# First feed-forward product with one 512-column pass per weight block, its halves summed at eviction, and conditioning units spread over two stages

## The reference

```
hn = rms_norm(h, g_ffn_pre[i])
f_gate, f_up = jnp.split(hn @ w_ffn_in[i], 2, axis=-1)      # 1024 -> 2 x 2816
f = (jax.nn.silu(f_gate) * f_up) @ w_ffn_out[i]             # 2816 -> 1024
h = h + rms_norm(f, g_ffn_post[i])
```

```
cond = jax.nn.silu(c)
mod = cond @ w_ada[layer] + b_ada[layer]                    # 1024 -> 6 x 1024
```

## Time and profile before

| | us |
|---|---|
| median of 3 runs | 1114.41 (1113.29 to 1114.71) |
| the profiled execution | 1109.89 |
| its span | 1108.1 |
| PE busy | 1014.9 (92%) |
| PEld busy | 764.6 (69%) |
| DVE busy | 505.7 (46%) |
| POOL busy | 493.3 (45%) |
| ACT busy | 379.1 (34%) |

### The profile page before, as it was taken

One profiled execution on the slowest core, in us unless ns is written; L12 is line 12 of the kernel. 1 busy time (PEld: TensorE's weight loads), 2 busy tenths in 40 slices (PEclk: granted clock), 3 DMA queues, 4 the chain that ended last, 5 costly groups with the idle time before them and its releaser, 6 DMA issues.

```text
span 1108.1 us, 18626 instructions
## 1 busy us (share of the span) xinstructions
PE 1014.9 (92%) x7938; PEld 764.6 (69%) x7938; DVE 505.7 (46%) x905; ACT 379.1 (34%) x540; POOL 493.3 (45%) x209
## 2 busy tenths in 40 slices
PE   7999999999999999999999999899988777878776
PEld 6989988788799999887898896344444333434332
DVE  2998987566457676214345544232232221212113
ACT  7345545643563344446595432000000000000002
POOL 6987799867786878988565510000000000000000
PEclk9999999999999999999999999999999999989999
DMA  9554455456569889858443879999999999999995
GB/s 366 210 190 156 154 191 208 166 202 235 197 250 336 313 348 360 314 190 331 133 151 121 326 322 419 413 426 425 427 427 425 425 427 426 427 427 424 425 424 210
DMA packets 38533, 342.07 MB, mean 309 GB/s; under 512 B 4273, under 2 KB 4657, under 8 KB 6322
## 3 DMA queue, kind: packets, MB, share of 16 engines
q1 hardware_dynamic: 37152, 337.56, 76.3%
q10 hardware_dynamic: 1298, 3.32, 0.9%
HBM read 339.81 MB, written 1.05 MB: 308 GB/s over the span
## 4 chain that ended last, share of the span: by engine, by line
PE 57%; DMA 26%; DVE 6%; POOL 6%; ACT 2%; SPq 2%; issue 1%; DVEq 0%; ACTq 0%; another core or an unknown queue 0%
DMA ring<-in_gu 17%; PE ps L521 12%; PE ps L523 12%; PE ps L522 12%; PE ps L1141 6%; POOL spl L2432 6%; DMA raw<-in_stream 5%; PE ps L1188 5%; DMA ring<-in_dn 3%; PE ps L1177 2%; SPq L2489 2%; PE ps L1121 1%; ACT sph L1245 1%; PE ps L514 1%; DVE ps L1960 1%
## 5 line engine op out<-in xcount | busy, mean ns | idle before, releaser
L2432 POOL TENSOR_TENSOR spl<-raw,sph 128x1024 fp32r<-128x1024 f32 x204 | 492.9, 2450 | 153.9 <-ACT sph L1245 153.9
L1245 ACT ACTIVATE sph<-raw 128x1024 fp32r<-128x1024 f32 x204 | 206.9, 1054 | 160.8 <-DMA raw<-in_stream 101.9
L521 PE MATMUL ps<-xbh,sph 128*128 128x256 f32 x480 | 137.0, 285 | 4.9 <-DVE xbl L1777 2.0
L522 PE MATMUL ps<-xbl,sph 128*128 128x256 f32 x480 | 136.0, 283 | 0.0
L523 PE MATMUL ps<-xbh,spl 128*128 128x256 f32 x480 | 136.0, 283 | 0.0
L2366 DVE TENSOR_TENSOR ar<-ar,ps 64x256 f32<-64x256 f32 x32 | 13.5, 423 | 262.2 <-ACT ar L1705 262.2
L1705 ACT ACTIVATE ar<-ps 64x256 f32<-64x256 f32 x32 | 12.1, 377 | 329.8 <-PE ps L1141 329.8
L1188 PE MATMUL ps<-ar,ar 128*128 128x512 f32 x256 | 119.8, 611 | 0.0
L521 PEld LDWEIGHTS ps<-xbh,sph 128*128 128x128 f32 x480 | 92.2, 192 | 6.3 <-DVE ar L2116 2.2
L521 PE MATMUL ps<-xah,sph 128*128 128x256 f32 x320 | 92.1, 288 | 1.1 <-DVE xal L1767 0.8
L522 PEld LDWEIGHTS ps<-xbl,sph 128*128 128x128 f32 x480 | 92.2, 192 | 0.0
(11 more groups left out here) (310 smaller groups left out, 1626.1 us busy)
## 6 DMA issues: line engine op xcount, KB each, us to landing
raw<-in_stream SPq DMA_DIRECT2D x127, 1024.0 KB, 5.1
ring<-in_gu SPq DMA_DIRECT2D x46, 2048.0 KB, 44.6
ring<-in_dn SPq DMA_DIRECT2D x22, 2048.0 KB, 44.6
ring<-in_gu SPq DMA_DIRECT2D x24, 1024.0 KB, 10.8
ring<-in_dn SPq DMA_DIRECT2D x14, 1024.0 KB, 9.2
ar<-in_gu SPq DMA_DIRECT2D x7, 1024.0 KB, 25.9
slotx<-in_gu SPq DMA_DIRECT2D x5, 1024.0 KB, 38.7
ar<-in_dn SPq DMA_DIRECT2D x3, 1024.0 KB, 47.8
```

Of the source, the lines that this page charges most:

```text
L521: e.matmul(o, sh, mh, start=start, stop=False)
L522: e.matmul(o, sh, ml, start=False, stop=False)
L1245: e.activation(u.half(SPH[u.n % NSP], h), u.half(RAW[u.slot], h), ACTF.Copy).then_inc(w.up(hi_ok), 1)
L2432: e.tensor_tensor(u.half(SPLO[u.n % NSP], h), u.half(RAW[u.slot], h), u.half(SPH[u.n % NSP], h), ALU.subtract).then_inc(w.up(lo_ok), 1)
```

## The change

- The planned stream has one ada unit in each of the 11 steps, two in steps 3 and 7 (13 instead of 20), and one ada unit before each of w0 to w8 (9 instead of 2).
- The activations' high and low parts (`XB`) become one tensor with a part index. `two_sided` takes the place of `fm_unit` for the gate and up units: per block one matmul of 512 columns (high weight times high and low activation side by side) and one of 256 columns (low weight times high activation) on top of the first half. A unit now fills a pair of banks, one bank for each half of 128 features, and each bank holds two partial results of 256 columns.
- DVE sums the partial results of each pair with a reduction over two elements (`ff_sum`): the gate's into `TMPF`, the up's into a new buffer `SUMU`. ACT's silu then works in place on `TMPF`, DVE multiplies `SUMU` into it (`ff_inner`), ACT and DVE take high and low part of it from there.
- DVE's order in step n is now: sum of the gate, `ff_low(n-1)`, the ada units that stand in the stream before step n+1, sum of the up, `ff_inner(n)`. ACT's order in step n: splits up to fg(n+1), `ff_high(n-1)`, silu, split of fu(n+1).

```diff
-        for _ in range(2 if n not in (0, 5) else 1):
+        for _ in range(2 if n in (3, 7) else 1):
             ada_unit()
     for c in range(11):
-        if c in (2, 4):
+        if c < 9:
             ada_unit()
...
+            def two_sided(v, name, xS, ready):
...
+                b = pair_of_banks(name)
+                claim(b)
+                claim(b + 1)
+                for h in range(2):
+                    c = slice(h * 128, h * 128 + 128)
+                    both = ps[b + h][:, :].rearrange("p (s n) -> p s n", s=2)
+                    w.wait_ge(lo_ok, 2 * u.n + h + 1)
+                    for k in range(8):
...
+                        e.matmul(both, H[:, k, c], xS[:, :, k, :], start=(k == 0), stop=False)
+                        mm = e.matmul(ps[b + h][:, 0:256], L[:, k, c], xS[:, 0, k, :], start=False, stop=(k == 7))
                     mm.then_inc(w.up(half_used), 1)
...
             for n in range(NFF // 2):
                 v = ff_at[n]
                 h = (n % 2) * 512
                 take(v)
-                w.wait_ge(half_used, 2 * units[v].n + 2)
-                if n >= 2:
-                    w.wait_ge(ffm_ok, lead(n - 2))
-                e.activation(TMPF[:, h:h + 512], ps[bank_of["fg", n]][:, :], ACTF.Silu).then_inc(w.up(ffa_ok), 1)
                 if n:
                     ff_high(n - 1)
...
+                w.wait_ge(ffm_ok, gate_summed(n))
+                e.activation(TMPF[:, h:h + 512], TMPF[:, h:h + 512], ACTF.Silu).then_inc(w.up(ffa_ok), 1)
                 take(v + 1)
...
+            def ff_sum(kind, n):
+
+                v = halves(bank_of[kind, n])
+                w.wait_ge(half_used, 2 * units[ff_at[n] + (kind == "fu")].n + 2)
+                to = k2(TMPF[:, (n % 2) * 512:(n % 2) * 512 + 512] if kind == "fg" else SUMU)
+                own()
+                e.tensor_reduce(to, v.rearrange("p h s n -> p h n s"), AX, ALU.add).then_inc(w.up(ffm_ok), 1)
+
+            def ff_inner(n):
+
+                t = TMPF[:, (n % 2) * 512:(n % 2) * 512 + 512]
+                w.wait_ge(ffa_ok, 2 * n + 1)
+                own()
+                e.tensor_tensor(t, SUMU, t, ALU.mult).then_inc(w.up(ffm_ok), 1)
+
             def ff_low(n):
 
-                w.wait_ge(ffa_ok, behind(n))
-                own()
-                e.tensor_tensor(FF[1][:, 2 * n:2 * n + 2, :], k2(ps[bank_of["fu", n]]), FF[0][:, 2 * n:2 * n + 2, :],
-                                ALU.subtract).then_inc(w.up(ffm_ok), 1)
+                w.wait_ge(ffa_ok, 2 * n + 2)
+                own()
+                e.tensor_tensor(FF[1][:, 2 * n:2 * n + 2, :], k2(TMPF[:, (n % 2) * 512:(n % 2) * 512 + 512]),
+                                FF[0][:, 2 * n:2 * n + 2, :], ALU.subtract).then_inc(w.up(ffm_ok), 1)
 
             m = 2
-            while ada_at[m] < ff_at[1]:
-                ada(m)
-                m += 1
             for n in range(NFF // 2):
-                f = ps[bank_of["fu", n]][:, :]
-                w.wait_ge(ffa_ok, lead(n))
-                w.wait_ge(half_used, 2 * units[ff_at[n] + 1].n + 2)
-                own()
-                e.tensor_tensor(f, f, TMPF[:, (n % 2) * 512:(n % 2) * 512 + 512], ALU.mult).then_inc(w.up(ffm_ok), 1)
+                ff_sum("fg", n)
                 if n:
                     ff_low(n - 1)
-                while m < len(ada_at) and ada_at[m] < (ff_at + wide_at[:2])[n + 2]:
+                while ada_at[m] < (ff_at + wide_at[:1])[n + 1]:
                     ada(m)
                     m += 1
+                ff_sum("fu", n)
+                ff_inner(n)
             ff_low(NFF // 2 - 1)
```

More of the change, by code:

```diff
@@ L221, in sem @@
             return ctx.enter_context(nc.semaphore(name))
-        ps = [ctx.enter_context(nc.psum_tensor(f"ps{i}", [128, 512], F32)) for i in range(8)]
+        banks = ctx.enter_context(nc.psum_tensor("ps", [128, 4096], F32))
+        ps = [banks[:, 512 * i:512 * i + 512] for i in range(8)]
         base = (nc.sbuf_base + 31) // 32 * 32
@@ L249, in program @@
         XA = tuple(k8(at(n, O_XA + 2048 * i, 2048, F32R)) for i, n in enumerate(("xah", "xal")))
-        XB = tuple(k8(at(n, O_XB + 2048 * i, 2048, F32R)) for i, n in enumerate(("xbh", "xbl")))
+        XBS = at("xb", O_XB, 4096, F32R).rearrange("p (s k n) -> p s k n", s=2, k=8)
+        XB = XBS[:, 0], XBS[:, 1]
         small_at, ar_n = [0], [0]
@@ L293, in program @@
         TMPF = at("tmpf", O_XA + 3072, 1024)
+        SUMU = ar(22000, 512)
         o_wr = const_at["mean"][0]
@@ L461, in x3, with halves, gate_summed, up_summed @@
             return X3 + 2 * PARTS.index(q) + 2
[L463 to L468, removed]
+        def halves(b):
+            return banks[:, 512 * b:512 * b + 1024].rearrange("p (h s n) -> p h s n", h=2, s=2)
+        def gate_summed(n):
+            return max(1, 4 * n)
+        def up_summed(n):
+            return 4 * n + 2
+        def inner_ok(n):
+            return 4 * n + 3
+        def low_done(n):
+            return min(4 * n + 5, 4 * (NFF // 2))
         def head(kind, h):
@@ L542, in fm_unit, with pair_of_banks @@
                                      xT[1][:, k, :], k == 0, k == 7)
+                    mm.then_inc(w.up(half_used), 1)
+                return b
+            def pair_of_banks(name):
+                if turn_at[0] % 2:
+                    turn_at[0] += 1
+                turn_at[0] %= 8
+                while turn_at[0] in held or turn_at[0] + 1 in held:
+                    turn_at[0] = (turn_at[0] + 2) % 8
+                b = bank(name)
+                bank((name, "next"))
+                return b
+            def two_sided(v, name, xS, ready):
+                u = units[v]
+                H, L = k8(SPH[u.n % NSP]), k8(SPLO[u.n % NSP])
+                b = pair_of_banks(name)
[6 more added lines that the diff above has]
+                    for k in range(8):
+                        if ready:
+                            w.wait_ge(*ready(k))
+                        e.matmul(both, H[:, k, c], xS[:, :, k, :], start=(k == 0), stop=False)
+                        mm = e.matmul(ps[b + h][:, 0:256], L[:, k, c], xS[:, 0, k, :], start=False, stop=(k == 7))
                     mm.then_inc(w.up(half_used), 1)
@@ L746, in tensor @@
             for n in range(NFF // 2):
[L747 to L750, removed]
+                b = two_sided(ff_at[n], ("fg", n), XBS, landed("norm2", 2))
+                free[b] = free[b + 1] = [(ffm_ok, gate_summed(n))]
+                b = two_sided(ff_at[n] + 1, ("fu", n), XBS, None)
+                free[b] = free[b + 1] = [(ffm_ok, up_summed(n))]
             bb = [bank(("f", j)) for j in range(4)]
@@ L768, in tensor @@
                         turn_x2(0)
-                    w.wait_ge(ffm_ok, behind(c))
+                    w.wait_ge(ffm_ok, low_done(c))
                     wide(wide_at[c], bb, [f[:, 2 * c:2 * c + 2, :] for f in FF], c == 0, c == 10, tt)
@@ L1469, in ff_high @@
             def ff_high(n):
-                w.wait_ge(ffm_ok, lead(n))
-                e.activation(FF[0][:, 2 * n:2 * n + 2, :], k2(ps[bank_of["fu", n]]), ACTF.Copy).then_inc(w.up(ffa_ok), 1)
+                w.wait_ge(ffm_ok, inner_ok(n))
+                h = (n % 2) * 512
+                e.activation(FF[0][:, 2 * n:2 * n + 2, :], k2(TMPF[:, h:h + 512]), ACTF.Copy).then_inc(w.up(ffa_ok), 1)
             for n in range(NFF // 2):
```

## The result

| | before | after |
|---|---|---|
| median, us | 1113.85 (4 runs, 1108.86 to 1114.71) | 1149.09 (4 runs, 1147.53 to 1149.48) |
| profiled execution | 1109.89 | 1149.37 |
| its span | 1108.1 | 1147.6 |

The changed kernel takes 1.033 of the time before (95% interval 1.031 to 1.035). The forecast was 1148 us, with a range of 1121 to 1162.

A forecast was written before the change was run, and what follows sets the result against it. The load stream, tied in a ring through DVE, was taken as the bound, not PE: 1109.9 + 13.6 (first half) + 20.0 (second) = 1143.5 us profiled; with the median 4.5 above, 1148 us, range 1121 to 1162.

The forecast's parts named there:

- The ring: First half, per step: load, ACT's split, `ff_high`, `ff_low`, ada unit, next load; 12.35 us against PE's 11.1.
- A(0): Moment DVE has done the ada unit of step 0, freeing its raw buffer for a load; forecast at 321.5 us.
- step 3: First-half step with two ada units: second load lands later, second unit and a transpose and reduction follow; 7.3 us extra.
- A(8): Moment DVE has done the ada work of step 8; eight turns and two extras after A(0), forecast at 433.4 us.
- The port: `ff_low`, both operands in SBUF, waits for the running POOL operation: 0.95 us; rival without this wait 1136 us, chance 0.20.
- PE's gain: Gate and up units: 0.347 us per block instead of 0.36, 4.7 us over 22 units if PE stays the bound.
- The sums: DVE's reductions of 1024 elements from pairs of partial results: 1.6 us each, on the path only in A(0).
- The start: PE's first gate unit waits for ACT's first PLE copy to free the second bank, some 0.5 us behind the old start.
- S: Moment PE starts the first gate unit of the first half, forecast at 311.1 us.
- The second half: Waits of PE before w0 (3.6), w1 (6.9), w3 (4.9) and at w8 to w10 (4.6): together 20.0 us more.
- The clock: PE's idle stretches of 3 us and more may lower its clock; 0 to 2 us, not in the sum.
- The offset: The median of the runs lies 4.5 us above the profiled execution, added to its 1143.5 us.

The follow-up runs named there:

- e4: The changed kernel with the ada unit ahead of `ff_low(n-1)` instead of behind it in DVE's program: 1123.6 us, ratio 1.009.
- h1: The changed kernel with DVE taking the ada units of step n+1 at the end of step n: 1120.8 us, ratio 1.008.
- e3: The changed kernel with the up unit's sum and the product in an idle PSUM bank instead of SBUF: 1139.1 us, ratio 1.0215.
- g3: The changed kernel with the product in PSUM, right operand in one stretch, ada units one step earlier, spread 16 and 6: 1114.2 us, ratio 1.0016.
- e1: The kernel before with only the new spread of ada units (13 in the first half, 9 in the second): 1119.8 us, ratio 1.0055.
- g1: The changed kernel with the product in PSUM, right operand in one stretch, ada units one step earlier, spread 20 and 2: 1113.8 us, ratio 1.0028.
- e5: e4 with the activations laid out block by block, so the right operand is one stretch: 1124.9 us, ratio 1.010.
- f1: e3 and e4 together, with the ada units spread 16 over the first half and 6 over the second: 1120.9 us, ratio 1.0066.
- g2: As g1, but with 18 ada units in the first half and 4 in the second: 1117.5 us, ratio 1.0046.

## Why the prediction was right, point by point

- **The ring.** Forecast 12.35 us per step. SP's issues behind A(0) to A(9) stand at 322.8, 334.9, 347.4, 366.7, 379.0, 391.4, 403.6, 421.4, 433.6 and 445.9: 12.1 to 12.5 in the plain steps, 19.3 for step 3 (forecast 19.65) and 17.8 for step 7 (18.15). A(8) was forecast at 433.4. Two small errors cancel in that: A(0) came 1.2 us late (forecast 321.5), and the eight steps behind it took 110.8 us for 111.9. e4 and h1 change the order alone and the first half falls by 18 and 20 us. Shown.
- **The port.** Forecast 0.95 us of waiting in `ff_low`: measured 1.505 - 0.69 = 0.8 in the median. e3 shows the cause; it shows less than the forecast made of it, 4.7 us in the first half where nine turns of 0.95 would be 8.6.
- **PE's gain.** Forecast 0.347 us per block and 4.7 us. Measured were 0.347 in nine units of the changed kernel and 0.353 in most others, 0.349 in the median of single blocks, so 352 x 0.011 = 3.9 us: mis-sized by 0.8 us. In g3, all at 0.353, it is some 2.4 us; there the first half falls by 3.1, with PE's 1.6 us of waits gone too and a stretch at the lower clock at its start that costs 1.7.
- **The sums.** Forecast 1.6, measured 1.225 us: nearer to the row with neighbouring elements.
- **The start.** S was forecast at 311.1, measured 310.9, but behind it the clock was at its lower level for 3.4 us.
- **The second half.** w0's first matmul: worked out 456.9, measured 456.8 (the last paragraph of the prediction said 453, which is where the first half's matmuls end). w1: worked out 469.2, measured 468.9. w3: 485.0 and 486.4. The shift at the end of the second half: worked out 33.6, measured 537.5 - 500.8 = 36.7 us.
- **The clock**, which I left out of the sum and put at 0 to 2 us, is the term that was wrong. In the second half three stretches at the lower level hold 15.2 us of PE's busy time and cost half of it, 7.6 us. They took the place of waits: before w1 4.9 us and not 6.9, before w3 3.6 and not 4.9, at w9 and w10 3.2 and not 4.6 (PE's idle time plus 0.16 each, since the last matmul before a wait is busy for 0.39 us where the next would start after 0.23). "The next stall hides it" held for 4.6 of the 7.6, and 3.0 are left, which is the difference between 33.6 and 36.7.
- **The offset.** I expected the profiled execution at 1143.5 and the median 4.5 above. The profiled execution took 1149.4 and lies at the median. Of the 5.9 us between, 3.1 are the shift above and 0.3 lie between the feed-forward and the expert stage; 2.5 arose in the expert stage, which took 423.7 us in the profile before and 426.3 after with the same instructions, and why is open. The 4.5 came from one profiled execution of the kernel before that was faster than the three runs it was compared with; in later sessions that kernel's median was 1111.9 to 1113.0. That the median was hit within 1.1 us is so partly luck: a sum too small by 5.9 and an offset too large by 4.8. The step, the path and the order of size were not luck.

## What to carry to other kernels

A unit's place in an in-order engine program is also the time at which its buffer comes free. Before moving an operation behind a wait, write down the ring: which load needs the buffer, what is split from it, what waits for the split, and what stands in front of the operation; sum it, and compare it with the step of the engine that sets the pace. Here an order with the same instructions cost 28 us. And spreading a side load over a stage at its limit only moves the loss, as e1 and g1 to g3 show. To look for a stage whose stream and PE both have slack is the next thing to try; no run here did.

## What the runs showed of the hardware

- A wait of PE of 2.32 us at the start of the first half was followed by 3.4 us at the lower clock level in the changed kernel; the 1.73 us there before were not. Four waits of 3.2 to 5.4 us each went with 6.8 us of it, twice as long as the stretch at 857 us of the earlier trace rows, one of 3.1 us with 3.4. The length of the wait alone doesn't decide: waits of 1.83, 1.88 and 1.94 us (g1, e5, g3) were followed by 3.4 us of it, waits of 2.00, 2.07 and 2.40 us (before, f1, g2) by none.
- The blocks of one 512- and one 256-column matmul ran at 0.347 or 0.353 us, whole units at a time. Both paces occur with the right operand in one stretch and in two.
- A DVE tensor-tensor operation on 128x512 with both operands in SBUF took 0.69 us when no POOL operation ran, and up to 2.89 us when one did: in the changed kernel, e4 and h1, 36 of the 37 that started while a POOL operation ran ended 0.54 to 0.56 us after that operation's end. With one operand in PSUM it took 0.69 to 0.70 us each time.
- Of two loads of 1 MB issued 0.4 us apart, the first landed 4.8 us and the second 6.9 us after its issue, so 2.5 us apart.
- Reducing pairs from PSUM, 1024 to 512 elements with 1 KB between the two, takes 1.225 us, the time of the 1024 neighbouring elements in SBUF in the earlier trace rows.
